# HGRN2's input projections computed ahead of SSD's in a four-branch recurrent decoder layer

## The chip, the cores and the metric

The kernel runs on one core of one Trainium2 chip. The metric is the device time of one execution in microseconds (us). The engines are PE (TensorE, matrix products), DVE (VectorE), ACT (ScalarE), POOL (GpSimd) and SP (SyncE, which here only issues DMAs). Each engine has a program of its own and works it off strictly in order; semaphores tie the programs together.

## The reference

One step of one decoder layer (width 1024) for 512 prompt tokens and for 8 samples of 4 tokens, 544 columns in all.

- `h = rms(x) * (1 + sc1) + sh1`, with shifts, scales and gates from `silu(c) @ ada_w`.
- `proj = h @ w_in`. Its columns feed four causal mixers of width 256: A, the gated delta rule (GDN); B, HGRN2; C, Mamba-2 SSD; D, mLSTM.
- A: `q, k, v = silu(conv4(...))`, q and k normalised per head; in chunks of 64 a unit lower triangular system is solved, `o = (q e^g) S + (q k^T * dec) u`, and `S` is carried to the next chunk.
- B: `kg = (1 - lb) sigmoid(-f)`, `logf = log(lb + (1 - lb) sigmoid(f))`, cumulative sums `g` per channel inside a chunk, `o = (q e^g) S + a v` with `a[l, m] = sum_c q_lc k_mc e^(g_lc - g_mc)`, and `S` carried.
- C: `x, B, C = silu(conv4(...))`, then `o = (C e^g) S + (C B^T * dec) v`. D: the same shape with a stabiliser `m` and a normaliser `n`.
- The four outputs are normalised and gated, lifted to 1024, merged with sigmoid gates from `h`, and projected by `w_out`; residual; then a SwiGLU FFN of width 2816, residual, final norm. The final recurrent states of prompt and samples are outputs too.

## The kernel before

The time falls into three stages: the first modulation and norm (to about 75 us), the window in which the mixers run (to about 529 us), and the wide products (gates, branch lifts, `w_out`, FFN) to the end. The change lies in the window.

**Units.** The input projection is cut into 15 groups of 256 columns of `w_in` (`GROUP_COLS`), and each group into 4 units: one of its two tiles of 128 features by one half (272) of the columns, with 8 products over k. `MIX_ORDER` lists the groups in the order in which they are computed: 0 to 2 are GDN's q, k, v; 3 its output gate; 4 to 6 HGRN2's q, f, i; 7 its gate; 8 SSD's gate; 9 and 10 SSD's x, B, C; 11 to 13 mLSTM's q, k, v; 14 its gate. From the sixth group on, units of the second modulation (`ada` and `turn`) are mixed in, 76 units in all, numbered 0 to 75 in `SEQUENCE`. SP loads the weights of a group when the one four loads before has been used. PE computes a unit in two halves (`part0`, `part1`) into one of two PSUM banks, ACT copies it out (L1413; L1415 and L1418 for the modulation), and PE may start unit u only when ACT has read unit u - 2.

**Chains.** The mixers are three chains of stages, each stage on one engine, each waiting for the one before it in its chain: `g` (GDN), `h` (HGRN2), `s` (SSD, and after it mLSTM). Every chain starts with preparation and then takes the prompt in four tiles of 128 columns and the samples as a fifth tile. GDN's preparation is `g_tail`, six convolutions (`g_conv`) with `g_silu`, and the norm of q and k: `g_l2sq` (DVE), four times `g_l2_n` (PE) and `g_l2r n` (ACT, L1428 and L1430: Ln, then Exp), `g_l2m` (DVE, L1764). HGRN2's is `h_silu` (ACT, L1465 and L1467: Sigmoid, then Silu), `h_lb6`, and for each of two tiles of f the stages `h_ls` (ACT), `h_b` (DVE), `h_ln` (ACT), `h_g` (DVE, scans at L1895 and L1896); `h_ls` and `h_ln` are Abs, Exp and Ln at L1475, L1477 and L1479. SSD's is `s_tail`, four `s_conv` and `s_silu` (L1514). A GDN tile is `g_tokens` (PE), `g_scale`, `g_bcast`, `g_diff`, `g_decay` (ACT, L1435), `g_kk` (PE), `g_lower` (DVE), `g_first` and then levels `g_x`, `g_xc`, `g_y`, `g_upd`. The sample tiles of GDN and HGRN2 end with long DVE stages, `g_utc` and `h_outc` (they spread a block over the 8 samples, L1926), and `g_statec` and `h_statec` (L1649 and L1932).

**What sets the order.** `shared_order` is a list scheduler that runs when the kernel is built. It knows a cost for every stage (`COSTS`, `SAMPLE_COSTS`) and the units that a stage needs (`NEEDS`). At every step it takes the stage that could start first, less a small credit for the chain with most work left, and fills PE with a unit where no stage could start sooner:

```
start = max([free[eng], ready[c]] + needs)
rank = start - WEIGHT * left[c]
...
if known and (best is None or start < best[0]):
    best = (start, "x", unit, f"part{part_}", "pe")
```

The result is one fixed program for PE, ACT and DVE. Behind it, ACT copies `hT` to its high parts (L1533, eight tiles, written over GDN's scratch) at the place where `g_statec` stands in the list, then makes the high part of the first gate weights (L1542); DVE waits for the ends of all three chains, makes the low part (L2260) and the low parts of `hT` (L2265), and PE's first gate product waits for those.

Of the kernel before, what the change touches and what calls it, by code (L numbers as in the profile page):

```python
# [38 lines left out]
SLOT = 2048  # L39


MIX_ORDER = [0, 1, 2, 9, 10, 4, 5, 6, 11, 12, 13, 3, 8, 7, 14]
GROUP_COLS = [0, 256, 512, 768, 1032, 1288, 1544, 1800, 2056, 2312, 2568, 2832, 3088, 3344, 3600]
C_GB, C_GA, C_DT, C_MI, C_MF, C_GATE = 1024, 1028, 2824, 3856, 3860, 3864

# [150 lines left out]
SEQUENCE = []  # L196
for _n in range(len(MIX_ORDER)):
    SEQUENCE += [("mix", 4 * _n + _v) for _v in range(4)]
# [7 lines left out]
def units_through(f):  # L206

    return POS[("mix", 4 * MIX_ORDER.index(f // 2) + 2 * (f % 2) + 1)] + 1

# [104 lines left out]
def trunk(nc, A, O):  # L314

    ctx = ExitStack()
    with ctx:
# [215 lines left out]
        def _(sp):  # L533
# [10 lines left out]
            def load(kind, slot, idx):  # L544

                full = ring[:, slot, :]
                if kind in ("ada1", "ada2", "mixer", "wout"):
                    src = kp({"ada1": "ada_w", "ada2": "ada_w", "mixer": "w_in", "wout": "w_out"}[kind])
                    if kind == "mixer":
                        c0 = GROUP_COLS[MIX_ORDER[idx]]  # L550
                    else:
# [819 lines left out]
        def _(act):  # L1371
# [35 lines left out]
            def read_unit(u):  # L1407
# [3 lines left out]
                if kind == "mix":  # L1411
                    f, h = 2 * MIX_ORDER[v // 4] + v // 2 % 2, v % 2
                    act.activation(pj[:, f, h * HN:(h + 1) * HN], ps[:, u % 2, 0:HN], ACT.Copy).then_inc(x_read, 1)  # L1413
# [1064 lines left out]
```

## Time and profile before

| | |
|---|---|
| device time, median of 3 runs (lowest, highest) | 1304.09 us (1301.78, 1304.91) |
| device time of the profiled execution | 1303.92 us |
| its span | 1302.1 us |
| PE busy | 1216.4 us (93%) |
| DVE busy | 566.2 us (43%) |
| ACT busy | 363.5 us (28%) |
| mean granted clock of PE | 0.965 of full speed |

The span is what the trace covers; the device time of the same execution is 1.8 us longer. A PE that is busy is not always at full clock: the granted clock is shown beside it, 1.00 being 2.4 GHz and 0.50 being 1.2 GHz.

### The profile page before, as it was taken

How to read it: one execution, taken by the hardware profiler on the slowest of the kernel's cores; microseconds unless marked ns; L12 is line 12 of the kernel's file. 1: busy time of each engine (PE TensorE's matmuls, PEld its weight loads, DVE VectorE, ACT ScalarE, POOL GpSimd, SP SyncE). 2: the span in 40 equal slices, each digit the busy share in tenths (PEclk: the TensorE clock that was granted, in tenths of full speed). 3: DMA queues.
4: the chain of work that ended last, by engine and by line, in shares of the span. 5: the costliest groups of instructions: out<-in, count | busy, mean ns of one | idle time of the engine just before them, and what ended most of it. 6: DMA issues, size and time to landing. Idle time of an engine off the chain costs nothing. (4 is left out here: it accounts for less than half of the span.)

```text
span 1302.1 us, 25005 instructions
## 1 busy us (share of the span) xinstructions
PE 1216.4 (93%) x10797; PEld 1088.2 (84%) x10797; DVE 566.2 (43%) x1166; ACT 363.5 (28%) x529; POOL 11.6 (1%) x30
## 2 busy tenths in 40 slices
PE   5599989989999999889999999969999999989997
PEld 2378767767787777789999998959999999989996
DVE  1352765556567775453333335462222222353322
ACT  2332371362121110561222221142222222331111
POOL 0000110000000000000000000000000000000000
PEclk9799999989999988889999999979999999989999
DMA  9813633113333211664333322212332332223201
GB/s 307 251 35 78 119 99 99 39 61 99 99 98 99 66 36 33 131 104 135 82 82 82 87 92 65 80 50 65 97 89 72 97 96 56 72 84 90 70 21 69
DMA packets 191026, 116.70 MB, mean 90 GB/s; under 512 B 36650, under 2 KB 189351, under 8 KB 190678
## 3 DMA queue, kind: packets, MB, share of 16 engines
q1 hardware_dynamic: 190358, 115.22, 32.0%
q8 instruction: 71, 1.16, 0.4%
q0 software_dynamic: 576, 0.14, 0.1%
q14 instruction: 21, 0.17, 0.0%
HBM read 108.38 MB, written 6.96 MB: 89 GB/s over the span
## 5 line engine op out<-in xcount | busy, mean ns | idle before, releaser
L741 PE MATMUL ps<-scr_parts 128*128 128x272 f32 x2688 | 522.6, 293 | 19.1 <-DVE hT_parts L2358 8.8
L741 PEld LDWEIGHTS ps<-scr_parts 128*128 128x128 f32 x2688 | 429.6, 191 | 23.9 <-issue 13.6
L741 PE MATMUL ps<-hT_parts,scr_parts 128*128 128x272 f32 x1408 | 391.2, 291 | 0.0
L2260 DVE TENSOR_TENSOR scr_parts<-ring,scr_parts 128x1024 fp32r<-128x1024 f32 (+1 forms) x100 | 128.9, 1289 | 308.8 <-ACT scr_parts L1542 305.8
L741 PEld LDWEIGHTS ps<-hT_parts,scr_parts 128*128 128x128 f32 x1408 | 262.0, 190 | 0.0
L741 PE MATMUL ps<-hT,ring 128*128 128x272 f32 x960 | 246.5, 409 | 3.0 <-ACT pj L1413 3.0
L1542 ACT ACTIVATE scr_parts<-ring 128x1024 fp32r<-128x1024 f32 (+1 forms) x100 | 111.0, 1111 | 493.2 <-PE ps L741 492.4
L741 PEld LDWEIGHTS ps<-hT,ring 128*128 128x128 f32 x960 | 182.3, 196 | 44.0 <-issue 3.2
L741 PE MATMUL ps<-pj_parts,scr_parts 128*128 128x272 f32 x992 | 169.2, 295 | 5.7 <-DVEq L1669 5.7
L741 PEld LDWEIGHTS ps<-pj_parts,scr_parts 128*128 128x128 f32 x992 | 143.2, 192 | 7.3 <-DVEq L1669 6.3
L741 PE MATMUL ps<-scr 64*64 64x64 f32 (+6 forms) x2024 | 82.7, 236 | 2.8 <-ACT scr L1442 2.3
L741 PEld LDWEIGHTS ps<-scr 64*64 64x64 f32 (+4 forms) x2024 | 61.4, 134 | 27.5 <-issue 21.5
L1413 ACT ACTIVATE pj<-ps 128x272 f32<-128x272 f32 x60 | 23.7, 394 | 139.1 <-PE ps L741 138.9
L2307 DVE TENSOR_TENSOR Rr<-pj,ps 128x544 f32<-128x544 f32 x16 | 11.5, 721 | 62.7 <-PE ps L741 62.4
L741 PE MATMUL ps<-pj 128*128 128x272 f32 (+3 forms) x260 | 38.7, 318 | 0.0
L741 PEld LDWEIGHTS ps<-pj 128*128 128x128 f32 (+3 forms) x260 | 28.7, 169 | 6.8 <-issue 2.1
L745 PE MATMUL ps<-cst,pj 128*128 128x128 f32 (+4 forms) x123 | 21.1, 283 | 13.7 <-DMA cst<-in_const_dram 6.2
L741 PE MATMUL ps<-pj,kg 128*128 128x272 f32 (+2 forms) x200 | 33.6, 333 | 0.0
L745 PEld LDWEIGHTS ps<-cst,pj 128*128 128x128 f32 (+4 forms) x123 | 13.7, 142 | 21.0 <-DMA cst<-in_const_dram 6.2
L741 PEld LDWEIGHTS ps<-pj,kg 128*128 128x128 f32 (+2 forms) x200 | 24.9, 168 | 6.0 <-issue 1.9
L741 PE MATMUL ps<-ring,scr 128*32 128x256 f32 x384 | 25.9, 395 | 1.5 <-DMA ring<-in_ada_w_dram 1.5
L1739 DVE SCALAR_TENSOR_TENSOR scr<-pj,vt,scr 128x511 f32<-128x511 f32 (+2 forms) x30 | 22.5, 750 | 2.3
(310 smaller groups left out, 974.0 us busy)
## 6 DMA issues: line engine op xcount, KB each, us to landing
ring<-in_w_in_dram SPq DMA_DIRECT2D x62, 512.0 KB, 6.8
ring<-in_ada_w_dram SPq DMA_DIRECT2D x48, 512.0 KB, 6.6
ring<-in_ffn_w_in_dram SPq DMA_DIRECT2D x44, 512.0 KB, 4.6
ring<-in_ffn_w_out_dram SPq DMA_DIRECT2D x16, 384.0 KB, 3.6
ring<-in_ffn_w_out_dram SPq DMA_DIRECT2D x16, 320.0 KB, 4.1
ring<-in_w_out_dram SPq DMA_DIRECT2D x8, 512.0 KB, 4.8
x_scratch<-scr SPq DMA_DIRECT2D x1, 2176.0 KB, 13.3
Q<-x_scratch SPq DMA_DIRECT2D x1, 2176.0 KB, 11.3
```

The source lines that it names most:

```text
L741: return pe.matmul(out, lhsT, rhs, start=start, stop=stop, skip_group_check=True)
L745: return pe.transpose(out, in_, ident[0:n, 0:n])
L1413: act.activation(pj[:, f, h * HN:(h + 1) * HN], ps[:, u % 2, 0:HN], ACT.Copy).then_inc(x_read, 1)
L1542: act.activation(hi, src, ACT.Copy).then_inc(w_split_hi, 1)
L1739: dve.scalar_tensor_tensor(out=acc[:, d:T], in0=pj[:, f, 0:T - d], scalar=w_[k], in1=acc[:, d:T], op0=MUL, op1=ADD)
L2260: dve.tensor_tensor(lo, src, hi.bitcast(F32), SUB).then_inc(w_split, 1)
L2307: dve.tensor_tensor(two(Rr[:, :]), gate_t, lift, MUL).then_inc(lin_read, 1)
```

## The change

Groups 4, 5 and 6 (HGRN2's q, f, i) move in front of groups 9 and 10 (SSD's x, B, C). Nothing else is edited: the same products, stages and DMAs are issued. GDN and HGRN2 both already work in chunks of 64.

```diff
-MIX_ORDER = [0, 1, 2, 9, 10, 4, 5, 6, 11, 12, 13, 3, 8, 7, 14]
+MIX_ORDER = [0, 1, 2, 4, 5, 6, 9, 10, 11, 12, 13, 3, 8, 7, 14]
```

Since `NEEDS` now lets HGRN2's chain start at unit 24 instead of unit 36 (units numbered from 0), and SSD's convolutions after unit 36 instead of unit 19, the scheduler writes another order for all three engines. Three places of it follow.

ACT, from the second `g_l2r` on, in the kernel before; L1514 is `s_silu` and L1413 a unit's copy:

```order
L1428 ACT_TABLE_LOAD
L1428 ACTIVATE scr<-ps,colp 128x544
L1430 ACT_TABLE_LOAD
L1430 ACTIVATE scr<-scr 128x544
L1514 ACT_TABLE_LOAD
L1514 ACTIVATE pj<-scr 128x544
L1413 ACTIVATE pj<-ps 128x272
```

The same place now, from `h_silu` on (L1465, L1467), with the last `g_l2r`, then `h_ls0` and the start of `h_ln0`:

```order
L1465 ACT_TABLE_LOAD
L1465 ACTIVATE kg<-pj 128x544 x2
L1467 ACT_TABLE_LOAD
L1467 ACTIVATE pj<-pj 128x544 x2
L1418 ACTIVATE mod<-ps 128x36
L1428 ACT_TABLE_LOAD
L1428 ACTIVATE scr<-ps,colp 128x544
L1430 ACT_TABLE_LOAD
L1430 ACTIVATE scr<-scr 128x544
L1413 ACTIVATE pj<-ps 128x272
L1475 ACTIVATE scr<-pj 128x544
L1477 ACTIVATE scr<-scr 128x544
```

SSD's Silus stood between GDN's norms; now HGRN2's preparation stands there and behind, one stage between two unit copies.

PE, the first GDN tile, in the kernel before, from `s_bcast` (Rr, 128x128) and `g_tokens` (cst,pj and Er, Vr) to `g_bcast` (Rr, 64x64), `s_e` and `g_kk` (scr,pj):

```order
L741 MATMUL ps<-Rr,cst 128x128 x8
L745 MATMUL ps<-cst,pj 128x128 x4
L741 MATMUL ps<-Er,cst 64x128 x2
...
L741 MATMUL ps<-hT,ring 128x272 x8
L741 MATMUL ps<-pj 128x128 x2
L745 MATMUL ps<-cst,pj 128x128 x3
L741 MATMUL ps<-Rr,cst 64x64 x8
L741 MATMUL ps<-hT,ring 128x272 x8
L741 MATMUL ps<-Er,cst 64x128 x8
L741 MATMUL ps<-scr,pj 64x64 x8
```

The same place now, from the two units ahead of `g_tokens`; the 32x256 row is an `ada` unit:

```order
L741 MATMUL ps<-hT,ring 128x272 x16
L745 MATMUL ps<-cst,pj 128x128 x4
L741 MATMUL ps<-Er,cst 64x128 x2
...
L741 MATMUL ps<-hT,ring 128x272 x8
L741 MATMUL ps<-Rr,cst 64x64 x8
L741 MATMUL ps<-ring,scr 32x256 x16
L741 MATMUL ps<-hT,ring 128x272 x8
L741 MATMUL ps<-scr,pj 64x64 x8
```

SSD's first stages are gone from it; between `g_tokens` and `g_kk` three units stand, with only `g_bcast` among them.

PE, the end of the window before, from `h_tok` (cst,scr 32x128 x1) on; scr,Q rows are the products with the 8 sample states, 64x512 rows are `g_state` and `h_state`, and hT,ring rows are units, the last being unit 75:

```order
L745 MATMUL ps<-cst,scr 32x128
L745 MATMUL ps<-cst,pj 32x128
L741 MATMUL ps<-hT,ring 128x272 x4
L741 MATMUL ps<-scr 64x32 x4
L741 MATMUL ps<-scr,Q 64x4 x32
L741 MATMUL ps<-scr 64x32 x4
L741 MATMUL ps<-scr,Q 64x4 x32
L741 MATMUL ps<-scr 64x512 x4
L741 MATMUL ps<-hT,ring 128x272 x4
L741 MATMUL ps<-scr 64x512 x4
L741 MATMUL ps<-scr_parts 128x272 x2
```

The end now, from the last unit on:

```order
L741 MATMUL ps<-hT,ring 128x272 x4
L741 MATMUL ps<-scr 32x32 x12
L741 MATMUL ps<-pj 32x32 x4
...
L741 MATMUL ps<-scr 64x32 x8
L741 MATMUL ps<-scr,Q 64x4 x32
L741 MATMUL ps<-scr 64x32 x4
L741 MATMUL ps<-scr,Q 64x4 x32
L741 MATMUL ps<-scr 64x512 x4
L745 MATMUL ps<-cst,scr 32x128 x2
L741 MATMUL ps<-scr 64x32 x4
L741 MATMUL ps<-scr,Q 64x4 x32
```

After this last row comes `g_state`, and then the gate products. Before, one stage of a chain (`h_state`) stood behind the last unit; now twelve do, nearly the whole sample tile of GDN and most of HGRN2's, and GDN's `g_state` is last instead of HGRN2's `h_state`. DVE's list ends accordingly: before `g_outc`, `h_outc`, `g_statec`, `h_statec`; now `h_outc`, `g_uc`, `h_statec`, `g_utc`, `g_outc`, `g_statec`.

## Rows read from the trace of the kernel before

**Rows 1.** The page's line of busy time by engine

```profile
PE 1216.4 (93%) x10797; PEld 1088.2 (84%) x10797; DVE 566.2 (43%) x1166; ACT 363.5 (28%) x529; POOL 11.6 (1%) x30
```

**Rows 2.** Stretches: length, busy by engine (instructions), granted PE clock, DMA share, GB/s

```profile
158.00:304.00 146.00, 131.72 (x1632) 101.49 (x1631) 87.26 (x226) 67.68 (x96) 4.61 (x9) 0.96 0.25 81
304.00:510.00 206.00, 203.02 (x2916) 157.76 (x2915) 134.18 (x397) 36.72 (x98) 0.00 (x0) 0.98 0.25 74
510.00:523.40 13.40, 13.38 (x112) 7.72 (x110) 5.82 (x10) 3.03 (x6) 0.00 (x0) 0.62 0.06 9
512.00:520.00 8.00, 8.00 (x53) 4.63 (x53) 5.07 (x8) 0.00 (x0) 0.00 (x0) 0.50 0.01 2
183.40:186.60 3.20, 2.97 (x7) 2.27 (x8) 2.56 (x4) 3.15 (x5) 0.00 (x0) 0.50 1.02 325
```

**Rows 3.** Timeline of PE: start, length, what, [idle before, releaser]

```profile
81.12 22.27 PE L741 MATMUL ps<-hT,ring 128*128 128x272 f32 x96
...
160.29 1.18 PE L741 MATMUL ps<-scr,cst 128*128 128x272 f32 x4 [1.66 <-DVEq L1669]
...
171.69 1.93 PE L741 MATMUL ps<-ring,scr 128*32 128x256 f32 x32
...
183.63 3.62 PE L741 MATMUL ps<-hT,ring 128*128 128x272 f32 x8 [2.96 <-ACT pj L1413]
...
264.56 0.69 PE L741 MATMUL ps<-Rr,cst 96*32 96x32 f32 x16 [2.61 <-DVEq L1669]
```

**Rows 4.** Timeline of ACT in the preparation of GDN and of HGRN2

```profile
179.28 1.28 ACT L1428 ACT_TABLE_LOAD   x1
...
181.34 1.28 ACT L1430 ACT_TABLE_LOAD   x1
182.64 0.66 ACT L1430 ACTIVATE scr<-scr 128x544 f32<-128x544 f32 x1
...
259.93 1.20 ACT L1467 ACTIVATE pj<-pj 128x544 f32<-128x544 f32 x2
...
271.13 0.65 ACT L1475 ACTIVATE scr<-scr 128x544 f32<-128x544 f32 x1
...
275.12 0.66 ACT L1479 ACTIVATE scr<-scr 128x544 f32<-128x544 f32 x1
```

**Rows 5.** Timeline of DVE in the same preparation

```profile
183.33 2.63 DVE L1764 SCALAR_TENSOR_TENSOR pj<-pj,scr 128x544 f32<-128x544 f32 x4 [0.31 <-ACT scr L1430]
...
275.81 0.50 DVE L1654 TENSOR_SCALAR scr<-scr,hcol 128x544 f32<-128x544 f32 x1 [3.37 <-ACT scr L1479]
...
278.68 0.20 DVE L1896 TENSOR_TENSOR_SCAN pj<-cst,scr 128x32 f32<-128x32 f32 x1
```

**Rows 6.** Timeline of all engines at the end of the window

```profile
508.43 2.03 PE L741 MATMUL ps<-scr,Q 64*64 64x4 f32 x64
...
510.74 3.38 PE L741 MATMUL ps<-scr,Q 64*64 64x4 f32 x64
...
514.05 3.67 PE L741 MATMUL ps<-scr 32*64 32x512 f32 x8
...
514.64 2.49 DVE L1926 TENSOR_TENSOR scr<-scr,cst 32x512 f32<-32x512 f32 x4
...
519.08 1.22 DVE L1932 TENSOR_TENSOR Q<-Q,ps 128x1024 f32<-128x1024 f32 x1
520.37 4.48 ACT L1533 ACTIVATE scr_parts<-hT 128x544 fp32r<-128x544 f32 x8 [14.06 <-DVEq L1669]
...
521.45 1.93 PE L741 MATMUL ps<-scr 32*64 32x512 f32 x8
...
525.03 2.04 ACT L1542 ACTIVATE scr_parts<-ring 128x1024 fp32r<-128x1024 f32 x2
...
526.88 1.23 DVE L2260 TENSOR_TENSOR scr_parts<-ring,scr_parts 128x1024 fp32r<-128x1024 f32 x1 [0.17 <-issue]
...
528.88 0.79 PE L741 MATMUL ps<-scr_parts 128*128 128x272 f32 x2 [5.50 <-DVE hT_parts L2265]
```

## The prediction, written before the changed kernel ran

> **What bounds the kernel now.** I read the page first: PE is busy for 93% of the span, DVE for 43% [rows 1]. Since the change issues the same products, it can move the time only through what PE loses in the window: idle time, and time at half clock. So I cut the window into stretches and took length less PE busy. From 158 to 304 us, where GDN, SSD and HGRN2 are prepared, PE idles 14.3 us; from 304 to 510 us, where the chains run beside units, 3.0 us; from 510 to 523.4 us nothing [rows 2]. Then it waits 5.5 us for the first gate product [rows 6]. The clock costs too: a half of a product's time is lost where the granted clock is 0.50, that is 1.2 GHz. The stretch of 8 us from 512 on has it with PE busy throughout [rows 2]; at a clock of 0.62 the 13.4 us of that end lose 5.1 us. One 3.2 us stretch behind the wait of 2.96 us has it too [rows 2, 3], and the product there takes 3.62 us for half a unit, where six full units take 22.27 us, 3.7 each [rows 3]. Mean clocks of 0.96 and 0.98 in the two long stretches put the loss there at about 5 and 3 us.
>
> So before: body (158 to 510) 17.3 us idle and 8 at half clock; end 5.5 idle and 5 at half clock. The sum below is made against the profiled execution (span 1302.1, time 1303.92 us), which lies 0.2 under the median of 1304.09; I add the difference to the median.
>
> **Part 1, the preparation.** Removed from here: four SSD convolutions, and four Silus that each forced a table load between GDN's Ln and Exp. Added: HGRN2's preparation, some 100 us earlier. I followed ACT, since unit u waits for the copy of unit u - 2. Durations: a `g_l2r` takes 4.0 us (179.28 to 183.30), `h_silu` two loads and twice 1.20, 5.0 us, an `h_ls` or `h_ln` 4.65 us (271.13 to 275.78), and 3.4 where the Exp table is there already [rows 4]. `g_l2m` is 2.63, `h_g` 3.1 (275.81 to 278.88) [rows 5].
>
> - `g_l2_0` still waits for DVE's squares, which come at 160.3 as before; the wait is 0.8 instead of 1.66 us [rows 3], since unit work stands where SSD's tail was not ready.
> - The three later norms are covered by units (3.7 us each) or by an `ada` unit (1.93 [rows 3]): no wait.
> - PE ends unit 24 at about 174.5, and then has the last norm product and a `turn` (1.0 each) and two units, to 184.0. ACT meanwhile has the copy, `h_silu` and the last `g_l2r`, to 184.35; `g_l2m` lands at 187.0 and `g_tokens` waits for it: 3.0 us.
> - Then `g_kk` waits for `g_decay`, which ACT reaches only behind `h_ls0`, `h_ln0` and `h_ls1`, and these wait for DVE in between. From the end of the last `g_l2r`: 0.4 copy, 3.4 `h_ls0`, 2.0 `h_b0`, 4.65 `h_ln0`, 0.4 copy, 3.1 `h_g0`, 4.65 `h_ls1`, 0.6 copy, 1.7 `g_decay` with its load: 20.9 us with handovers, to about 205. PE has in that time the 3.0 us wait, `g_tokens` and `g_bcast` (2.2), two units (7.4) and an `ada` (1.9): it is there at 199. Wait: 6 us. Queued behind it are a `turn`, unit 32 and `g_first`.
> - Then SSD's four convolutions come, 3.7 us of DVE each, between levels of GDN and HGRN2. I followed `g_upd5`, `g_uc0` and `s_silu3` behind them; the units placed there cover all but 1.4 us.
>
> Sum to unit 44: 0.8 + 3.0 + 6.0 + 1.4 = 11.2 us idle against 14.3, and two half clock stretches instead of three, 3.4 against 5.1 us lost. Gain 4.8 us. Bounds: nothing gained if each stage misses its slot as in the kernel before, and 9 us if the 6 us wait shrinks to the 2.6 us that the longest one there lasted [rows 3], and takes its half clock stretch along.
>
> **Part 2, from unit 45 to unit 75.** Before, from 304 us on, one or two of the chains run in much of it. Now SSD's tiles 1 to 4 come beside GDN's and HGRN2's second tile, all feeding on DVE, which was busy 65% there [rows 2]. Idle 3.0 us before is the lower end; at the rate of the busy first stretch (14.3 of 146) 100 us of crowding give 9.8 and the rest 2, some 12 us. The units between the stages are the same as in the stretch with 3.0, so I lean to it: 6.5 us. Loss 3.5 us (0 to 9). The half clock stretch near 470 stays.
>
> **Part 3, the end.** This decides. Before, units 72 to 75 stand among the last stages of GDN and HGRN2; now they are issued ahead, and behind unit 75 (call its end E) PE has only the two sample tiles, which hand over between PE, ACT and DVE. Steps on the path from E: small stages to `h_tok`'s copy 3.9 us (an estimate, eight handovers of half a microsecond); `h_out` 2.4 (0.4 and 2.03 [rows 6]); `h_outc` 3.0 (2.49 for the spread [rows 6]); `h_state` 1.95; `h_statec` 2.5 (two of 1.22); `g_utc` 3.0; `g_out` 2.4; `g_outc` 0.5; `g_state` 1.95; `g_statec` 2.5. That is 24.1 us. Behind it ACT copies the eight tiles of `hT`, 4.48 us; they were made while PE and DVE worked on HGRN2, and HGRN2's end hid them: `g_statec` was over at 520.3 and `h_statec` at 526 [rows 6]. That cover is gone because GDN is last now, and they write into GDN's scratch. Then one high part (1.0) and 2.0 us from the low part's start to PE's (526.88 to 528.88) [rows 6]. E to the first gate product: 24.1 + 0.2 + 4.5 + 1.0 + 2.0, with handovers 32 us.
>
> The PE pieces of this at half clock: `h_out` took 3.6 us and the state product 3.67 [rows 6]. With all of them so, 6.6 us more, 38.6. The same kind of sequence fell to 0.50 at 511 without an idle gap, and here there are gaps, so I take 36.
>
> Of these 36 us PE works 13.2 at full clock (three times 2.4, two times 1.95, 2.1 of small ones), so 22.8 are lost (18.8 to 25.4). Before, 5.5 + 5.0 were. Part 3 costs 12.3 us (8.3 to 15).
>
> **Sum.** -4.8 + 3.5 + 12.3 = +11.0: 1304.1 + 11.0 = 1315 us. The gate stage and the FFN, 773 us from 528.9 on, are untouched; SP's stores start relatively earlier there, and the wait they could shorten is set by ACT's norms, not by them.
>
> On table loads the rows show 1.28 us, and the activation 0.02 us behind it (181.34, 182.64) [rows 4]. The Trainium skill, ScalarE: Activation LUTs, section "What ACT_TABLE_LOAD costs", puts about 1.38 us of drain on top, 2.66 per switch. The trace does not show it. By the page the ten loads from `h_silu` to `g_decay` would cost 13.8 us more.
>
> **Rivals.**
>
> - B, not slower. The end costs less than it seems and the preparation gains more: the body's 14.3 us of idle and 5 at half clock were made by GDN's norms and SSD's Silus alternating on ACT; if HGRN2's stages fit between the units, up to 9 us come back there, and with the end at full clock (8.3) and part 2 at nothing the time is 1304.1 - 9 + 8.3 = 1303.4. It decides from the point at which the wait before `g_kk` is under about 2 us. For it: ACT has two loads fewer in its program. Against it: the end has no unit left, whatever the preparation does.
> - C, crowding. DVE becomes the bound between units 45 and 54, where an SSD, a GDN and an HGRN2 tile want it at once: 12 instead of 6.5 us idle, and one or two half clock stretches of 1.7: 1323 us. For it: DVE's share was already 65%; against: idle was only 3.0 then.
> - D, longer table switches. If each of the ten switches held ACT for as long again as its load (1.28), the waits before `g_tokens` and `g_kk` grow by 12.8 us, to 1328. The page named above says so; [rows 4] speak against it.
>
> **How the numbers follow.** A, as worked out, 0.64, with its own range 1308 to 1320. B 0.17, of which 0.10 falls within 0.3% (3.9 us, about what a measurement of this kernel can tell from no change) and 0.07 below. C 0.16, D 0.03. Slower 0.64 + 0.16 + 0.03 = 0.83. The range leaves out the lower half of B and the upper parts of C and D, about 0.18: 1305 to 1323.
>
> **What would show it.** Right: unit 75's copy near 505 us and the first gate product near 540; DVE stages of GDN last before it, then eight copies of `hT` on ACT with PE idle for about 10 us; `g_tokens` waiting 3 us and `g_kk` 6 us, near 185 and 200. Half clock through most of the end. Wrong: a body with over 25 us idle (C), a `g_kk` that doesn't wait (B), or a gate product under 30 us behind unit 75.

## The result, and the profile after

The changed kernel takes 1313.92 us in the median of 4 runs (1310.51 to 1316.22), where the kernel before, measured beside it, takes 1304.1 (1301.78 to 1304.91): ratio 1.0078, 95% interval [1.0061, 1.0095], 9.8 us slower. The profiled execution is the fastest of the four, 1310.51 us with a span of 1308.7; against the profiled execution of before it is 6.6 us longer, and it lies 3.4 us under its own median.

The line of busy time, to be held against [rows 1]:

```profile
PE 1218.4 (93%) x10797; PEld 1090.0 (83%) x10797; DVE 566.6 (43%) x1166; ACT 360.8 (28%) x527; POOL 11.6 (1%) x30
```

Little is to be seen there: the same products, two table loads of ACT fewer, 2 us more of PE. Where the time went shows in the stretches of the window. The columns are those of [rows 2]; the third stretch begins where unit 75 ends, the fourth ends at the first gate product.

```profile
158.00:304.00 146.00, 137.84 (x1514) 105.95 (x1516) 81.54 (x219) 67.56 (x104) 4.60 (x9) 0.96 0.30 95
304.00:497.60 193.60, 190.32 (x2872) 147.97 (x2865) 134.19 (x387) 32.37 (x82) 0.00 (x0) 0.98 0.23 67
497.60:530.20 32.60, 23.00 (x278) 15.44 (x278) 13.79 (x27) 1.26 (x5) 0.00 (x0) 0.54 0.28 68
530.20:537.67 7.47, 0.00 (x0) 0.03 (x1) 2.46 (x4) 7.44 (x11) 0.00 (x0) 0.50 0.53 103
537.67:1308.70 771.03, 740.32 (x5490) 722.41 (x5490) 273.29 (x372) 207.51 (x249) 0.00 (x0) 0.97 0.30 79
```

Length less PE busy gives the idle time: 8.2 us in the preparation where before had 14.3, then 3.3 for the rest of the body (the stretch up to unit 75; before 3.0), and 9.6 and 7.5 at the end, where before had 5.5. The first gate product comes at 537.67 instead of 528.88, 8.8 us later. Idle up to it grew from 22.8 us to 28.5; the other 3 us are products at half clock, PE busy from 158 us on being 351.2 instead of 348.1 us.

The end on the timeline of all engines, to be held against [rows 6]. Columns: start, length, engine, line, operation, and in brackets the idle time before it and what ended it.

```profile
497.62 0.40 ACT L1413 ACTIVATE pj<-ps 128x272 f32<-128x272 f32 x1 [1.22 <-PE ps L741]
...
502.15 3.58 PE L741 MATMUL ps<-scr,Q 64*64 64x4 f32 x64
...
506.22 3.58 PE L741 MATMUL ps<-scr,Q 64*64 64x4 f32 x64
506.25 2.49 DVE L1926 TENSOR_TENSOR scr<-scr,cst 32x512 f32<-32x512 f32 x4
...
509.73 3.67 PE L741 MATMUL ps<-scr 32*64 32x512 f32 x8
...
514.76 1.22 DVE L1932 TENSOR_TENSOR Q<-Q,ps 128x1024 f32<-128x1024 f32 x1
...
516.59 2.48 DVE L1926 TENSOR_TENSOR scr<-scr,cst 32x512 f32<-32x512 f32 x4
...
519.16 0.64 PE L741 MATMUL ps<-scr 32*64 32x32 f32 x8 [5.22 <-DVEq L1669]
...
519.73 3.58 PE L741 MATMUL ps<-scr,Q 64*64 64x4 f32 x64
...
523.90 3.68 PE L741 MATMUL ps<-scr 32*64 32x512 f32 x8 [0.59 <-DVEq L1669]
...
528.93 1.22 DVE L1932 TENSOR_TENSOR Q<-Q,ps 128x1024 f32<-128x1024 f32 x1
...
530.21 4.48 ACT L1533 ACTIVATE scr_parts<-hT 128x544 fp32r<-128x544 f32 x8 [28.59 <-DVEq L1669]
...
535.67 1.23 DVE L2260 TENSOR_TENSOR scr_parts<-ring,scr_parts 128x1024 fp32r<-128x1024 f32 x1 [4.77 <-ACT scr_parts L1542]
...
537.67 0.79 PE L741 MATMUL ps<-scr_parts 128*128 128x272 f32 x2 [10.10 <-DVE hT_parts L2265]
```

Unit 75 is read at 497.62. All that follows belongs to the two sample tiles: three 64x4 groups at 3.58 us where full clock makes 2.03, one wait of 5.22 us for DVE (which finishes `h_statec` at 515.98 and only then makes GDN's spread), `g_statec` to 530.15, the eight copies of `hT` behind it, and 10.1 us of waiting PE.

The preparation, PE's timeline, to be held against [rows 3]:

```profile
159.83 1.18 PE L741 MATMUL ps<-scr,cst 128*128 128x272 f32 x4 [0.75 <-DVEq L1669]
...
186.66 1.12 PE L745 MATMUL ps<-cst,pj 128*128 128x128 f32 x4 [2.79 <-DVEq L1669]
...
189.61 5.52 PE L741 MATMUL ps<-hT,ring 128*128 128x272 f32 x16
...
204.26 0.46 PE L741 MATMUL ps<-scr,pj 64*64 64x64 f32 x16 [2.79 <-ACT scr L1435]
```

The three waits of the forecast (0.8, 3.0, 6.0) are there, with 0.75, 2.79 and 2.79 us. The third depends on the execution: e5 below has the same instructions in this stretch and shows it with 5.72 us.

### The profile page after: what moved, and what is told of

Read it like the earlier page. It is cut to its first block and busy times, and to the rows that moved or that the text cites. A ratio compares the mean times of both kernels' runs of the same rounds, so it can differ in the third digit from the quotient of the medians.

```text
span 1308.7 us, 25002 instructions
## 1 busy us (share of the span) xinstructions
PE 1218.4 (93%) x10797; PEld 1090.0 (83%) x10797; DVE 566.6 (43%) x1166; ACT 360.8 (28%) x527; POOL 11.6 (1%) x30
## 5 line engine op out<-in xcount | busy, mean ns | idle before, releaser
L741 PE MATMUL ps<-scr_parts 128*128 128x272 f32 x2688 | 521.6, 293 | 23.1 <-DVE hT_parts L2265 10.1
L741 PEld LDWEIGHTS ps<-scr_parts 128*128 128x128 f32 x2688 | 429.1, 191 | 28.3 <-issue 13.6
L741 PE MATMUL ps<-hT_parts,scr_parts 128*128 128x272 f32 x1408 | 390.9, 291 | 0.0
L741 PEld LDWEIGHTS ps<-hT_parts,scr_parts 128*128 128x128 f32 x1408 | 261.6, 190 | 0.0
L741 PE MATMUL ps<-hT,ring 128*128 128x272 f32 x960 | 240.1, 402 | 0.1
L741 PEld LDWEIGHTS ps<-hT,ring 128*128 128x128 f32 x960 | 178.7, 192 | 38.1 <-issue 1.5
L741 PE MATMUL ps<-pj_parts,scr_parts 128*128 128x272 f32 x992 | 168.8, 295 | 5.7 <-DVEq L1669 5.7
L741 PEld LDWEIGHTS ps<-pj_parts,scr_parts 128*128 128x128 f32 x992 | 142.8, 191 | 7.3 <-DVEq L1669 6.3
L741 PE MATMUL ps<-scr 64*64 64x64 f32 (+7 forms) x2024 | 84.5, 239 | 8.2 <-DVEq L1669 7.3
L741 PEld LDWEIGHTS ps<-scr 64*64 64x64 f32 (+4 forms) x2024 | 62.1, 135 | 31.0 <-issue 16.8
L1413 ACT ACTIVATE pj<-ps 128x272 f32<-128x272 f32 x60 | 23.7, 394 | 143.5 <-PE ps L741 143.2
L741 PE MATMUL ps<-pj 128*128 128x272 f32 (+3 forms) x260 | 38.9, 319 | 1.2 <-ACT scr L1520 0.9
L745 PE MATMUL ps<-cst,pj 128*128 128x128 f32 (+4 forms) x123 | 22.2, 292 | 15.6 <-DMA cst<-in_const_dram 6.0
L741 PEld LDWEIGHTS ps<-pj 128*128 128x128 f32 (+3 forms) x260 | 28.7, 169 | 7.4 <-ACT scr L1520 1.4
L745 PEld LDWEIGHTS ps<-cst,pj 128*128 128x128 f32 (+4 forms) x123 | 14.1, 145 | 23.9 <-DMA cst<-in_const_dram 6.0
L741 PE MATMUL ps<-pj,kg 128*128 128x272 f32 (+2 forms) x200 | 33.8, 331 | 0.0
L741 PEld LDWEIGHTS ps<-pj,kg 128*128 128x128 f32 (+2 forms) x200 | 25.0, 168 | 4.3 <-issue 0.2
L741 PE MATMUL ps<-ring,scr 128*32 128x256 f32 x384 | 25.7, 394 | 1.4 <-DMA ring<-in_ada_w_dram 1.4
```

The costliest lines, as they stand in the source:

```text
L741: return pe.matmul(out, lhsT, rhs, start=start, stop=stop, skip_group_check=True)
L745: return pe.transpose(out, in_, ident[0:n, 0:n])
```

## The experiments

Theory 1 is the forecast's: the loss is the stretch behind the last unit, in which only chains of dependent steps are left. The kernels below vary that end (what is placed in it, how much, which chain comes last, at which clock), the preparation, and the change itself by one group. Lines added to a kernel push its line numbers up: L745 in e1, e6 and e9 is L741 here. Those called "after" start from the changed kernel, those called "before" from the other. Medians are read against the kernel before in the same set of runs: 1304.44 us for the first four, 1304.11 for the next four, 1304.87 for the last four.

In the table, idle is length less PE busy from 158 us to the first gate product. "Extra busy" is PE busy there over the 348.1 us of before, less filling products: time lost at half clock, compared with what before loses. The column "4001st" is the start of PE's 4001st product, and the next one the time from it to the first gate product (e7 has its products in another order, so none is given).

| kernel | first gate product | 4001st | from it to the gate | idle | extra busy | median | ratio |
|---|---|---|---|---|---|---|---|
| before | 528.88 | 426.4 | 102.5 | 22.8 | 0 | 1304.1 | 1 |
| after | 537.67 | 420.2 | 117.4 | 28.5 | 3.0 | 1313.9 | 1.0078 |
| e1 after, last units later | 537.68 | 420.9 | 116.8 | 25.6 | 6.0 | 1314.5 | 1.0081 |
| e2 before, last units earlier | 537.51 | 426.6 | 110.9 | 30.5 | 0.9 | 1312.2 | 1.0054 |
| e3 after, no log | 536.15 | 417.2 | 118.9 | 25.7 | 4.3 | 1307.8 | 1.0023 |
| e4 after, filled | 539.83 | 424.6 | 115.3 | 17.1 | 3.6 | 1311.0 | 1.0052 |
| e5 after, GDN first | 537.50 | 422.8 | 114.7 | 27.0 | 4.4 | 1311.0 | 1.0047 |
| e6 after, eight units spread | 532.58 | 421.8 | 110.8 | 22.6 | 3.9 | 1305.3 | 1.0009 |
| e7 one group moved | 548.94 | | | 31.1 | 11.7 | 1324.5 | 1.0162 |
| e8 before, GDN first | 543.53 | 430.0 | 113.5 | 29.7 | 7.7 | 1314.7 | 1.0074 |
| e9 e6 filled | 534.32 | 421.3 | 113.1 | 19.1 | -2.0 | 1305.2 | 1.0001 |
| e10 before, filled | 528.93 | 426.4 | 102.5 | 18.9 | 0 | 1300.8 | 0.9970 |
| e11 before, unit 75 later | 530.36 | 425.8 | 104.6 | 21.5 | 2.8 | 1304.5 | 0.9997 |
| e12 before, no log | 525.79 | 421.8 | 104.0 | 19.8 | -0.1 | 1299.1 | 0.9949 |

One profile of a kernel may lie 3 us beside its median, as that of after does; the verdicts go by medians. The two middle columns show where such scatter arises. Up to the 4001st product after, e1, e4, e5, e6 and e9 run one and the same program, and yet their profiles reach it between 420.2 and 424.6 us, after first of all; before, e2, e8, e10 and e11 do so too, between 425.8 and 430.0 us, e8 last. So the place of a gate product by itself misleads: e4 and e5 are 2.2 and 2.8 us faster than after from the 4001st product on, though their gate products don't come earlier by as much, and 3.7 of the 14.6 us by which e8's gate product is late arose ahead of anything that its edit touches.

**e1_hold: after, its last four units held back.**

```
+HOLD = {(72,0): ("g",4,"g_x1"), (72,1): ("g",4,"g_qk"), (73,1): ("g",4,"g_sk"), (74,0): ("g",4,"g_u"),
+        (74,1): ("g",4,"g_ut"), (75,0): ("h",4,"h_tok"), (75,1): ("g",4,"g_state")}
 known = all(("x", n) in when for n in needs)
+if (unit, part_) in HOLD and HOLD[(unit, part_)] not in when:
+    known = False
```

> The changed kernel, but its last four units (72 to 75) are held back in the scheduler until named stages of the sample tiles have been issued, so that they stand again among those stages, the last of them behind GDN's state product. Nothing is left out. Theory 1 (the loss is the exposed end: 40 us from unit 75 to the first gate product against 7 before, with 13 us of PE work in it): 14.8 us of unit work at full clock moves into it, so 7 to 14 us come back: 1300 to 1307 us, and the first gate product starts at 525 to 531 us. Rival (the loss comes from the third chain being there all along, not from the end): the units only change places, 1311 to 1316 us.

Measured: 1314.51 us (8 runs), interval of the ratio [1.0055, 1.0107], in the rival's range, and the gate product at the same place as in after. Timeline of PE in this kernel:

```profile
476.96 3.68 PE L745 MATMUL ps<-scr 32*64 32x512 f32 x8 [1.37 <-DVEq L1673]
...
485.69 3.67 PE L745 MATMUL ps<-scr 32*64 32x512 f32 x8 [2.04 <-DVEq L1673]
...
493.15 0.42 PE L745 MATMUL ps<-scr,pj 64*32 64x32 f32 x8 [2.87 <-ACT scr L1439]
...
537.68 0.79 PE L745 MATMUL ps<-scr_parts 128*128 128x272 f32 x2 [6.51 <-DVE hT_parts L2269]
```

The units fill the end, and are missed where they came from: mLSTM's last steps and `g_kk` now wait, and the products around them fall to half clock. So theory 1 in its simple form (put the last units back and the time is back) fell.

**e2_rush: before, all remaining units placed at once as soon as `m_norm` is issued.**

```
-if known and (best is None or start < best[0]):
+if known and (best is None or start < best[0] or ("s", NT, "m_norm") in when):
```

> The kernel before, with one change: from the point at which mLSTM's last state product is issued, the rest of the units (half of 72 to 75) goes out at once, ahead of the remaining stages of GDN and HGRN2. The order of the groups is that of before, so the preparation and the body are untouched. Nothing is left out. Theory 1: the same exposed end without the new order, 8 to 15 us slower than before, 1312 to 1319 us. HGRN2's state comes last here, so the copies of hT stay covered and the end is about 5 us cheaper than in the changed kernel. Rival (the end costs nothing by itself): within 3 us of before.

Measured: 1312.21 us (12 runs), [1.0038, 1.0070]. The order of the groups, and all that goes with it, is that of before; only the end is bare. Timeline of PE:

```profile
490.98 13.10 PE L741 MATMUL ps<-hT,ring 128*128 128x272 f32 x56
...
512.65 0.63 PE L741 MATMUL ps<-scr 32*64 32x32 f32 x8 [3.16 <-DVEq L1669]
...
528.34 3.68 PE L741 MATMUL ps<-scr 32*64 32x512 f32 x8 [3.09 <-DVEq L1669]
```

Two waits for DVE's spread appear and the last state product is at half clock: 7.8 us, most of what the change costs, without the change.

**e3_noln: after, with HGRN2's log left out.** This kernel leaves the logarithm of HGRN2's gate out, and with it table loads: the page counts 519 instructions of ACT instead of 527, so that there are eight fewer and not the six that the expectation names.

```
-act.activation(x, x, ACT.Ln, bias=1.0).then_inc(hgrn_s, 1)
+act.activation(x, x, ACT.Abs, scale=0.01).then_inc(hgrn_s, 1)
```

> The changed kernel with the logarithm of HGRN2's preparation replaced by an absolute value (so the gate's log is left out and HGRN2's results differ): six table loads between the last g_l2r and g_decay go, 1.28 us each, 7.7 us of ACT. Theory 1 (the waits of 2.8 us before g_tokens and before g_kk are ACT's, and each puts PE at half clock for a few us behind it): the wait before g_kk goes and with it its half clock, the one before g_tokens stays; 3 to 5 us faster than the changed kernel. Rival (the preparation is bound by DVE or hidden anyway): within 1 us of the changed kernel.

Measured: 1307.82 us (12 runs), [1.0006, 1.0040], 6.1 us under after, more than the 3 to 5 of theory 1. The wait before `g_kk` is gone, that before `g_tokens` stays. Whether that is a part of the change's loss is asked again by e12.

**e4_fill: after, 5 and 14 products that nobody reads in two waits of the end.**

```
+rest.after(pe, NT, "m_normc")
+fill(5)            # mm(ps[:, 2, 0:HN], ones, cst[:, 0:HN]), n times
 gdn.begin(pe, t, "g_out")
...
+fill(14)
 h_parts = [h_hi[:, k, :] for k in range(KD)]
```

> The changed kernel with idle work added on PE at the end: 5 products of 128x272 with constants before GDN's last output products and 14 before the first gate product, into a bank that is free there. Nothing is left out. Theory 1 (half clock is what made the end 40 instead of 32 us): the clock comes back in the fill, the last output and state products take 2 instead of 3.6 us each and the gate stage starts at full clock: 3 to 5 us faster than the changed kernel. Rival (the clock doesn't follow the fill, or the fill itself delays): the same or up to 4 us slower, with the granted clock at 0.50 through it.

Measured: 1311.0 us (12 runs), [1.0034, 1.0069], 2.9 under after, just short of theory 1's 3 to 5; the interval touches that of after, [1.0061, 1.0095]. Timeline of PE:

```profile
523.43 2.03 PE L741 MATMUL ps<-scr,Q 64*64 64x4 f32 x64
526.06 3.67 PE L741 MATMUL ps<-scr 32*64 32x512 f32 x8 [0.59 <-DVEq L1676]
529.66 8.20 PE L741 MATMUL ps<-cst 128*128 128x272 f32 x28
539.83 0.49 PE L741 MATMUL ps<-scr_parts 128*128 128x272 f32 x2 [1.97 <-DVE hT_parts L2272]
```

`g_out` runs at full clock again (`g_state` behind it doesn't, at 3.67 us), and the gate stage starts at 0.49 us for a pair instead of 0.79. From the 4001st product to the gate it is 2.2 us less than in after, and behind the gate product 770.5 us instead of 771.0. About 3 of the 9.8 us are thus a price of the clock, and can be had back without moving a step.

**e5_gdn_first: after, GDN ahead of HGRN2 in the sample tile.**

```
-rank = start - WEIGHT * left[c]
+rank = start - WEIGHT * left[c] - (0.5 if c == "g" and t == NT else 0.0)
```

> The kernel after, with the delta rule's stages of the 64-row sample tile ranked 0.5 us ahead of the other chains' in the order of the kernel: its last stages g_sk to g_state now come ahead of HGRN2's h_qk1, h_tok, h_out and h_state on TensorE, and ahead of the same copies on VectorE. Theory 1 (the end is bound by the latency of the chain that comes last, the delta rule's, and by the 4.5 us of copies on ScalarE that can start only behind its last copy): those copies now run beside HGRN2's last stages, the first gate product comes 4 to 6 us earlier than 537.7, and the median is 1308 to 1310 us. Theory 2 (the end is bound by half-clock products and VectorE work whatever their order): the order trades one chain's wait for another's, first gate product within 1.5 us of 537.7, median 1312.5 to 1315.5.

Measured: 1311.02 us (6 runs), [1.0034, 1.0060], 2.9 under after: between the theories, outside both of their ranges, and so is the 2.8 us saved from the 4001st product to the gate. ACT and PE on the timeline, with the wait before `g_kk` first:

```profile
203.73 0.71 PE L741 MATMUL ps<-scr,pj 64*64 64x64 f32 x16 [5.72 <-ACT scr L1435]
...
523.98 4.48 ACT L1533 ACTIVATE scr_parts<-hT 128x544 fp32r<-128x544 f32 x8 [14.10 <-DVEq L1669]
...
528.32 3.68 PE L741 MATMUL ps<-scr 32*64 32x512 f32 x8 [3.09 <-DVEq L1669]
...
537.50 0.79 PE L741 MATMUL ps<-scr_parts 128*128 128x272 f32 x2 [5.50 <-DVE hT_parts L2265]
```

The copies do run beside HGRN2 now, and PE's last wait is 5.5 instead of 10.1 us: the cover of the copies is worth their 4.5 us. But HGRN2's state product, last now, waits 3.09 us for DVE's spread where GDN's had waited 0.59, which takes a good part of it back. The wait before `g_kk`, in a stretch that the edit does not touch, is 5.72 us here and 2.79 in the profile of after: the unit behind the wait of `g_tokens` ran at full clock in this execution (3.93 us), so PE came sooner and waited longer.

**e6_spread: after, eight units held back from tile 3 on.** The two lines of e1, with this table:

```
+HOLD = {(68,0): ("g",3,"g_x4"), (69,0): ("g",3,"g_y5"), (70,0): ("g",3,"g_out0"), (71,0): ("s",4,"m_den"),
+        (72,0): ("s",4,"m_state"), (73,0): ("g",4,"g_bcast"), (73,1): ("g",4,"g_first"), (74,0): ("g",4,"g_sk"),
+        (74,1): ("h",4,"h_state"), (75,0): ("h",4,"h_state"), (75,1): ("g",4,"g_state")}
```

> The kernel after, with units 68 to 75 held back from tile 3 on: unit 68 until g_x4 of tile 3 is placed, 69 until g_y5, 70 until g_out0, 71 until m_den of the sample tile, 72 until m_state, the halves of 73 and 74 until g_bcast, g_first, g_sk and h_state, and unit 75 until h_state and g_state. Theory 1 (chains' latency bounds the end, a unit held back only moves the wait): waits of 1 to 4 us appear between 440 and 500 us, the first gate product stays at 535 to 540, and the median is 1311 to 1317 us. Theory 2 (the end is bare of independent work, so work spread wider covers it): PE idle between 440 us and the first gate product falls from some 22 us to some 12, gate product at 527 to 531, median 1303 to 1308.

Measured: 1305.31 us (12 runs), [0.9999, 1.0019], no longer to be told from before: 8.6 of the 9.8 us are back, with the change's order of groups untouched. Timeline of PE:

```profile
502.01 0.64 PE L745 MATMUL ps<-scr 32*64 32x32 f32 x8 [3.10 <-DVEq L1673]
...
517.69 3.67 PE L745 MATMUL ps<-scr 32*64 32x512 f32 x8 [3.08 <-DVEq L1673]
521.30 7.86 PE L745 MATMUL ps<-hT,ring 128*128 128x272 f32 x24
...
532.58 0.79 PE L745 MATMUL ps<-scr_parts 128*128 128x272 f32 x2 [3.42 <-DVE hT_parts L2269]
```

Twenty-four products of units stand between the last chain step and the gate stage. From 440 us to the first gate product PE idles 12.0 us (92.6 less 80.6), as theory 2 had it; after had 17.1 there (97.7 less 80.5) and not the 22 that it started from, and the gate product itself came later than it said. Taken from a longer stretch than in e1, the units cover the end and are hardly missed before. So the loss is for the most part a matter of where the last eight units stand.

**e7_one_group: a part of the change.**

```
-MIX_ORDER = [0, 1, 2, 4, 5, 6, 9, 10, 11, 12, 13, 3, 8, 7, 14]
+MIX_ORDER = [0, 1, 2, 9, 4, 5, 6, 10, 11, 12, 13, 3, 8, 7, 14]
```

> Part of the change alone: the groups run 0, 1, 2, 9, 4, 5, 6, 10, so that group 9 stays ahead of HGRN2's groups and only group 10 goes behind them. HGRN2's preparation starts one group (4 units, 23 us) later than in the kernel after and one earlier than before. In the written order unit 75 now ends ahead of the sample tile's m_state and g_tokens, farther from the end than in either kernel. Theory 1 (the loss is the stretch behind unit 75): more of it is bare than after, so the median is 1315 to 1322 us, with the first gate product at 540 to 546. Theory 2 (the loss comes from moving HGRN2's preparation, in proportion): the median lies between the two kernels, 1307 to 1311 us.

Measured: 1324.51 us (5 runs), [1.0145, 1.0179], beyond theory 1's 1322: half of the change costs twice as much as the whole. Unit 75 ends at about 496.2 as in after, but more of the chains is left behind it: to the first gate product it is 52.7 us, with 17.5 us idle and a mean clock of 0.54:

```profile
496.20:548.94 52.74, 35.21 (x408) 22.69 (x407) 30.57 (x71) 9.71 (x20) 0.00 (x0) 0.54 0.23 53
```

The gate product comes at 548.9, beyond the 540 to 546 forecast; more of the loss against before is half clock (11.7 us) than idle (8.3 us). The bare end isn't all of it. At a mean clock of 0.54 some 32 of its 35.2 busy us are at half clock, which with the idle time makes some 33 us lost behind unit 75 (an estimate from the row above), where after loses 26.9 (17.1 idle, 9.8 at half clock): 5 to 6 of the 10.6 us over after. The rest lies ahead, 3.5 us of it as idle time in the preparation (11.7 us against 8.2). That HGRN2's earlier preparation costs in proportion is refuted.

**e8_before_gdn_first: before, with e5's line, and units from 68 on placed only into gaps over 0.6 us.**

```
-if known and (best is None or start < best[0]):
+if known and (best is None or start < best[0] - (0.6 if unit >= 68 else 0.0)):
```

> The kernel before (its group order), with the delta rule's sample tile ranked 0.5 us ahead and units from 68 on placed only where PE would else be idle for over 0.6 us: g_state of the sample tile comes ahead of units 73 to 75, and HGRN2's h_tok, h_out and h_state are all that is left behind unit 75. Theory 1: the 4.5 us of copies behind g_statec go beside units 73 to 75, three HGRN2 steps stay bare; first gate product 3 to 7 us earlier than 528.9 and a median of 1297 to 1301 us, under both kernels. Theory 2 (what is taken from the end comes back as waits ahead of it, VectorE in the same order being late): waits of 1 to 4 us at 460 to 500 us, gate product at 527 to 531, median 1302 to 1306 us.

Measured: 1314.72 us, [1.0057, 1.0091], from 6 runs in two groups: three of 1311.9 to 1312.7 us with a mean granted clock of 0.958, three of 1316.7 to 1317.0 with 0.953, and the profile is of the second. Both theories missed by 8 us or more. What is left behind unit 75 is only three steps of HGRN2, but `h_state` waits 3.08 us for the spread, the gate stage 5.50, and 29.7 us are idle in all; PE had stood at half clock before that too (0.78 in the mean from 470 to 500 us, where before has 0.89). In the preparation, which the edit leaves alone, the mean clock is 0.93 where before has 0.96, and 3.7 us were lost by the 4001st product; the 11.0 us behind it are what the edit can have done. Ranking the last chain first moves the bare steps here, and does not cover them.

**e9_spread_fill: e6 with five filling products ahead of each of three waits.**

```
+fill(5)   # ahead of g_ut and h_state of the sample tile, and of the first gate product
```

> e6_spread with five 128x272 products whose result nobody reads ahead of each of the three waits of its end (g_ut and h_state of the sample tile, the first gate product). Theory 1 (what is left of the end is waits for VectorE with products at half clock between them, and TensorE kept at work is granted full clock): the 64x4 products behind the first filling take 2.0 us instead of 3.58, the gate stage starts at full clock, 2 to 4 us gained on 1305.3, median 1301.5 to 1303.5 us, about the kernel before. Theory 2 (the chains of VectorE and the copies carry the end whatever the clock): 1304 to 1307 us.

Measured: 1305.20 us (11 runs), [0.9992, 1.0010]: nothing gained on e6. The gate stage starts at full clock, but the chain ahead of it is no faster:

```profile
498.80 4.24 PE L745 MATMUL ps<-cst 128*128 128x272 f32 x10
506.36 0.64 PE L745 MATMUL ps<-scr 32*64 32x32 f32 x8 [3.10 <-DVEq L1681]
506.93 3.58 PE L745 MATMUL ps<-scr,Q 64*64 64x4 f32 x64
```

The clock fell under the first filling (0.53, 0.50 and 0.70 in its three parts), and the 64x4 products behind it are still at 3.58 us. The filling came ahead of small products on which the wait depends, and so delayed the chain instead of standing in the wait, which is 3.10 us as in e6. The second filling did win full clock back: HGRN2's state product behind it takes 1.93 us, and 3.67 in e6. From the 4001st product to the gate it is 2.3 us longer than in e6, and behind the gate product 769.7 us against 770.9.

**e10_before_fill: before, with eight filling products ahead of its first gate product.**

```
+fill(8)
 h_parts = [h_hi[:, k, :] for k in range(KD)]
```

> The kernel before with eight such products in the 5.5 us wait ahead of its first gate product. Theory 1 (the half clock behind that wait costs what the clock's rows say, some 3 us): the gate stage starts at full clock and the median falls by 1.5 to 3 us, to 1301 to 1302.6. Theory 2 (the clock is lost to the 64x4 products ahead of the wait and the gate stage waits for VectorE's h_lo in any case): 1303.5 to 1305.5 us.

Measured: 1300.83 us (7 runs), ratio 0.9970, [0.9959, 0.9981]: faster than both kernels, and by 4.0 us against before, more than theory 1's 1.5 to 3. Two stretches of it:

```profile
523.40:528.93 5.53, 3.90 (x18) 2.95 (x17) 4.91 (x6) 5.50 (x8) 0.00 (x0) 1.00 0.91 249
528.93:1299.00 770.07, 738.44 (x5490) 720.06 (x5490) 273.18 (x372) 206.76 (x248) 0.00 (x0) 0.98 0.31 81
```

The same wait, and the start of the gate stage, in the kernel before:

```profile
523.40:528.88 5.48, 0.00 (x0) 0.03 (x1) 4.91 (x6) 5.45 (x8) 0.00 (x0) 0.62 0.93 253
528.88:535.00 6.12, 6.12 (x27) 6.12 (x28) 6.10 (x10) 5.39 (x9) 0.00 (x0) 0.51 0.75 150
```

The gate product starts where it did, and everything behind it lasts 770.1 us instead of 773.2. The clock stays at 1.00 through the wait, where it fell in before. This filling stands in a wait for DVE and ACT that it cannot lengthen, which is the difference from e9.

**e11_before_hold: before, unit 75 held back** by e1's two lines.

```
+HOLD = {(75,0): ("g",4,"g_state"), (75,1): ("h",4,"h_state")}
```

> The kernel before with unit 75 held back: its first half until g_state of the sample tile is placed, its second until h_state. Theory 1 (independent work behind the last chain step covers the 5.5 us wait for the copies): PE idle ahead of the first gate product falls from 5.5 to some 2 us, of which 1 comes back ahead of g_out, median 1300 to 1303 us. Theory 2 (that work is missed just ahead, and the unit's half has to end before VectorE's addition to mod, which stands ahead of the copies): 1304 to 1307 us.

Measured: 1304.53 us (11 runs), [0.9988, 1.0006]; theory 2. The last wait is 3.42 instead of 5.50 us, 0.83 comes back ahead of a GDN step, and DVE's work for the gate stage begins 1.5 us later because it stands behind the reading of unit 75 (529.49 against 528.02 for the first `h_lo`).

**e12_before_noln: before, with e3's edit**, the log of HGRN2's gate left out.

> The kernel before with the change of e3_noln (the log of HGRN2's gate left out, six loads of ScalarE's table fewer). Theory 1 (with the groups of the change ScalarE's preparation ends the waits of TensorE around 200 us, and its loads cost more than before): gain on 1304.1 of 0 to 2.5 us. Theory 2 (the loads cost the same wherever HGRN2's preparation stands): a gain of 5 to 7 us as in e3_noln, median 1297 to 1299 us.

Measured: 1299.05 us (6 runs), ratio 0.9949, [0.9935, 0.9963], a gain of 5.8 us where e3 had 6.1. The gain is theory 2's 5 to 7 us (the median lies just over the upper end of its range). ACT's table loads around the log cost the same in either order of groups as far as the medians tell, which is to 2 or 3 us, so no part of the 9.8 us is seen to be theirs.

## Why the prediction was right

Predicted were 1315 us and a slower kernel; measured 1313.9. The direction and the mechanism came out as forecast. That the number is within 1.1 us is in part luck: the end cost more than its own upper bound, the stretch ahead of it less than forecast, and the profiled execution gives 6.6 us where the medians give 9.8.

**Part 3, the end, forecast +12.3 us (8.3 to 15).** From unit 75's end to the first gate product it was 40.1 us, against 36 forecast and 38.6 for all at half clock. With the forecast's 13.2 us of work in it, 26.9 are lost (idle 17.1 and 9.8 of half clock), and that is 16.4 more than the 10.5 of before: 4.1 over the forecast, and over the upper bound of 15. The mechanism is the one named: the path of HGRN2 and then GDN, the copies of `hT` behind `g_statec` (4.48 us, as priced) and a bare 10.1 us. Two sizes were off. The clock was 0.50 from about 500 us on, and I had taken 36 out of 32 to 38.6, though the rows of before spoke for the upper end; and the path from E to the end of `g_statec` was 32.5 us, where the listed steps at half clock gave 30.7. About 1.0 of these 1.8 us is a step that the path lacked: HGRN2's spread ended at 508.74, but `h_state` began at 509.73, behind the 64x4 products of `g_sk`, which stood ahead of it on PE at half clock. The other 0.8 are handovers. That the bare end by itself costs about this much is shown from both sides: e2 makes before lose 7.8 us by baring its end, and e6 takes 8.6 of the 9.8 us away by covering it. e7 bares more and loses 10.6 us more than the change, 5 to 6 of them there.

**Part 1, the preparation, forecast a gain of 4.8 us (3.1 of idle time, 1.7 of half clock).** To 304 us 8.2 us are idle instead of 14.3, a gain of 6.1; the mean clock is 0.96 as before, so the half clock did not shrink. `g_l2_0` and `g_tokens` waited as forecast (0.75, 2.79). `g_kk` was released at 204.2 us, forecast 205, but PE came at 201.5 and not at 199, for the most part since the unit behind the first wait ran at half clock (16 products in 5.5 us instead of 3.7), so the wait was 2.79 and not 6.0. I had counted the half clock stretch as a loss of its own and not as something that eats the next wait. The six profiles with this preparation bear it out: with that unit at 5.46 to 5.77 us the wait is 2.54 to 4.04, and in e5, with the unit at 3.93, PE came at 198.0 and waited 5.72, nearly the forecast's 6.0.

**Part 2, units 45 to 75, forecast a loss of 3.5 us (0 to 9).** This is the term that was most clearly too large: from 304 us to unit 75's end 3.3 us are idle, which is close to the lower bound of 3.0. DVE is busy 69% there (134.19 of 193.6), no more than a little above the 65% of before, and three chains side by side fill each other's gaps. Rival C, crowding, is out. Parts 1 and 2 together brought 7.6 us where the forecast had 1.3 (5.8 of it is idle time read from the rows, 1.8 is what is left over), the excess coming from no crowding and a shorter wait at `g_kk`.

In the profiled executions this makes -7.6 + 16.4 = 8.8 us, where the first gate product stands, less 2.2 behind it: 771.0 us against 773.2, where the forecast had that stretch untouched. The order of the groups is not what the traces show as its cause. The same products take 770.9 to 771.5 us in after, e3, e6, e7, e8 and e11, and 773.0 to 773.4 in before, e1, e2, e5 and e12. In the first six the half clock at the head of the gate stage is over 3.1 to 3.9 us behind the first gate product, in the other five 5.7 to 6.0; with a filled wait ahead (e4, e9, e10) there is none, and they take 769.7 to 770.5.

That is 6.6 us of span; the median over all runs is 9.8. The 3 us between the two are the scatter of the executions. The profile of after has the short value behind the gate product, 2 us less than e1 and e5, and reached the 4001st product ahead of all its five siblings, by 0.7 to 4.3 us. Its three other runs list a mean granted clock of 0.951 or 0.952 where it has 0.954: over 1310 us that is 2.6 to 3.9 us more lost to half clock where PE is busy throughout (an estimate from these clocks), much of the 2.9 to 5.7 us by which they are longer.

**Rival B** had its condition fulfilled in part, in this execution: the wait before `g_kk` came close to its 2 us and the preparation gained. It failed on its other half, an end at full clock. **Rival D**, longer table switches, is out: on ACT the loads behind one another read 181.95 for 1.28 us, and the activation follows at 183.25. The Trainium skill, ScalarE: Activation LUTs, section "What ACT_TABLE_LOAD costs", puts 2.66 us on a switch. By this figure of the Trainium skill, as an estimate, the eight loads fewer of e3 would free 21 us of ACT. The traces do not agree: ACT is busy 10.6 us less there (360.8 to 350.2 on the pages of the profile), eight times 1.28 being 10.3, and from 158 to 304 us of after no load stands over 0.06 us behind the activation ahead of it.

Of the signs named, the gate product near 540, the 10 us behind the copies, half clock through the end and the wait at 185 are there; unit 75 near 505 was 7.4 us early, and the 6 us wait at 200 was under half in this profile (5.72 us in e5's).

What stays open: e8's loss is located (waits of 3.1 and 5.5 us and a lower clock from 470 on) but not divided among its two edits. No run spreads eight units in the kernel before, so it is not shown that e6's gain belongs to the changed order alone; the one unit held back in e11 brought nothing there. And no run separates, inside the end of after, the idle time made by DVE's spread from the half clock that follows it.

## What to carry to other kernels

When independent work feeds a set of dependent chains, count what is left of the chains behind its last piece, and price that tail at half clock with every handover in it; moving an input earlier can empty the tail's cover, as it did here, even where the preparation gets better. Hold back work over a long stretch rather than only the last pieces: eight units spread brought 8.6 us, four held late brought nothing (number and place changed together). Read a difference of 3 us or less from medians, not from one profile against another; where two kernels share a stretch of program, measure from its end. A wait that another engine sets anyway can be filled with products that nobody reads, which gives the next stage full clock (here it made the kernel before 0.3% faster); ahead of a wait that the filling itself lengthens it gains nothing.

## What the runs showed of the hardware

In the kernel before, the granted clock fell to 0.50 at 511 us with PE busy by the trace without a gap, 11.00 of 11.00 us up to the fall and 10.30 of 10.30 behind it:

```profile
500.00:511.00 11.00, 11.00 (x182) 9.39 (x178) 5.41 (x15) 0.80 (x3) 0.00 (x0) 1.00 0.01 2
511.00:521.30 10.30, 10.30 (x78) 6.31 (x74) 5.38 (x8) 0.93 (x2) 0.00 (x0) 0.50 0.01 2
```

So being busy by the trace does not keep the clock. Ahead of that fall stand units with small products between them and, from 508.43 on, two groups of 64x4 products without a unit between. In after it fell at 500.0, behind 2.4 us with 1.47 busy, and stayed at 0.50 through a stretch that was busy throughout:

```profile
505.00:512.00 7.00, 7.00 (x92) 5.38 (x92) 3.37 (x8) 0.00 (x0) 0.00 (x0) 0.50 0.01 2
```

Large products that nobody reads kept full clock where it stood (e10) and won it back where it had fallen (e4: 0.53 from 529.7 to 533, then 1.00), but under e9's first filling it was lost.

In e7 half clock grew the loss by more (11.7 us) than idle time did (8.3 us). And executions of one and the same program differ in it. The mean granted clock of after's profiled run is 0.954, and its four runs spread over 5.7 us. Of before, 31 executions in the first set of runs lie between 1301.8 and 1306.5 us but for one, at 1315.3 with a mean granted clock of 0.916. The preparation of before and of e8 is one program, with a mean clock of 0.96 in one trace and 0.93 in the other.
